# First layer's gated convolution in row form, with the token shift done by transfers inside the chip

## The reference, cut to what matters

```
h = rms_norm(x, pre_norm[i]);  proj = h @ w_in[i]
x_in, gate_b, gate_c = split(proj[:, :4608], 3)      # 1536 channels each
u    = gate_c * x_in
conv[s, c] = sum over k = 0..2 of u[s - 2 + k, c] * w[c, k]    # u of tokens before 0 is 0
tok_out = gate_b * conv
cross_out = cross-attention of the tokens into mem (512 channels)
branch = concat(tok_out, cross_out) * silu(gate)
x = x + rms_norm(branch @ w_out[i], post_norm[i])
```

## Time and profile before

| what | value |
|---|---|
| median of three executions | 956.55 us |
| profiled execution | 955.9 us, span 954.1 us |
| TensorE busy | 943.2 us (99%) |
| VectorE busy | 630.6 us (66%) |
| ScalarE busy | 474.9 us (50%) |
| DMA queue of SyncE | 59.8% of 16 engines' span |
| chain that ended last | TensorE 98% of the span |
| mixer's matmuls | from 110 to 376 us of the span |
| output projection of the first layer | from 380 to 467 us |

### The profile page before, as it was taken

How to read it: one execution, slowest core, us unless ns; L and a number is a source line. 1 busy time by engine, 2 the same in 40 slices (tenths; PEclk the granted TensorE clock), 3 DMA queues, 4 the chain that set the end, 5 groups by cost and what they waited for, 6 DMA issues and landing times.

```text
span 954.1 us, 14081 instructions
## 1 busy us (share of the span) xinstructions
PE 943.2 (99%) x5148; PEld 810.9 (85%) x5148; DVE 630.6 (66%) x868; ACT 474.9 (50%) x726; POOL 1.2 (0%) x9
## 2 busy tenths in 40 slices
PE   8999999999999999999999999999999999999996
PEld 7888888888888888888888888888888888888885
DVE  5877665666666666655595546457878778886555
ACT  6767544444444443344465355345465465464541
POOL 0000000000000000000000000000000000000000
PEclk9999999999999999999999999999999999999998
DMA  9757466666666665665576646565655755746562
GB/s 337 235 168 261 153 186 197 200 191 190 191 185 194 184 191 189 208 192 190 181 230 191 196 133 208 168 201 167 202 175 160 219 167 165 218 136 212 188 192 91
DMA packets 148778, 182.31 MB, mean 191 GB/s; under 512 B 8128, under 2 KB 116992, under 8 KB 147968
## 3 DMA queue, kind: packets, MB, share of 16 engines
q1 hardware_dynamic: 147792, 177.25, 59.8%
q10 hardware_dynamic: 944, 4.49, 1.2%
HBM read 176.48 MB, written 2.10 MB: 187 GB/s over the span
## 4 chain that ended last, share of the span: by engine, by line
PE 98%; DVE 1%; DMA 0%; ACT 0%; issue 0%; DVEq 0%; SPq 0%; ACTq 0%
PE psum L370 40%; PE psum L371 20%; PE psum L431 10%; PE psum L433 10%; PE psum L432 10%; PE psum L382 1%; PE psum L450 1%; PE psum L607 1%; PE psum L475 1%; PE psum L458 1%; PE psum L383 1%; DMA raw_ring<-in_w_kv_mem_dram 0%; PE psum L579 0%; PE psum L467 0%; PE psum L590 0%; PE psum L589 0%
## 5 line engine op out<-in xcount | busy, mean ns | idle before, releaser
L370 PE MATMUL psum<-hT_split,hi_ring 128*128 128x512 f32 x1600 | 559.3, 395 | 0.0
L923 DVE TENSOR_TENSOR lo_ring<-raw_ring,hi_ring 128x1024 fp32r<-128x1024 f32 x318 | 384.9, 1223 | 247.0 <-ACT hi_ring L656 245.5
L656 ACT ACTIVATE hi_ring<-raw_ring 128x1024 fp32r<-128x1024 f32 x318 | 335.3, 1062 | 392.8 <-PE psum L371 257.4
L371 PE MATMUL psum<-hT_split,lo_ring 128*128 128x256 f32 x1600 | 444.2, 278 | 0.0
L370 PEld LDWEIGHTS psum<-hT_split,hi_ring 128*128 128x128 f32 x1600 | 300.0, 188 | 70.5 <-issue 2.0
L371 PEld LDWEIGHTS psum<-hT_split,lo_ring 128*128 128x128 f32 x1600 | 300.7, 188 | 0.1
L431 PE MATMUL psum<-hi_ring,branchT_split 128*128 128x512 f32 x256 | 99.9, 390 | 0.0
L433 PE MATMUL psum<-hi_ring,branchT_split 128*128 128x512 f32 x256 | 99.6, 389 | 0.0
L432 PE MATMUL psum<-lo_ring,branchT_split 128*128 128x512 f32 x256 | 99.6, 389 | 0.0
L433 PEld LDWEIGHTS psum<-hi_ring,branchT_split 128*128 128x128 f32 x256 | 48.0, 188 | 10.0
L431 PEld LDWEIGHTS psum<-hi_ring,branchT_split 128*128 128x128 f32 x256 | 48.1, 188 | 10.0
(11 more groups left out here) (185 smaller groups left out, 675.7 us busy)
## 6 DMA issues: line engine op xcount, KB each, us to landing
raw_ring<-in_w_in_dram SPq DMA_DIRECT2D x224, 512.0 KB, 4.5
raw_ring<-in_w_out_dram SPq DMA_DIRECT2D x64, 512.0 KB, 4.8
raw_ring<-in_w_kv_mem_dram SPq DMA_DIRECT2D x30, 512.0 KB, 4.8
layer_area<-layer_area SPq DMA_DIRECT2D x48, 64.0 KB, 3.2
stage_area<-in_mem_dram SPq DMA_DIRECT2D x8, 256.0 KB, 6.1
x_residual<-in_x_dram SPq DMA_DIRECT2D x2, 1024.0 KB, 8.4
x_residual<-in_x_dram ACTq DMA_DIRECT2D x1, 2048.0 KB, 9.9
layer_area<-in_post_norm_dram ACTq DMA_DIRECT2D x2, 1024.0 KB, 5.9
```

What stands on the lines that cost most here:

```text
L370: mm(o, hi[:, k, P * c:P * (c + 1)], X[:, kt, :], start=kt == 0, stop=False)
L371: last = mm(o[:, SEQ:], lo[:, k, P * c:P * (c + 1)], X[:, kt, 0:SEQ], start=False, stop=kt == KT - 1)
L656: run(whi[:, slot, :], raw[:, slot, :], ACT.Copy).then_inc(hi_ready, 1)
L923: V_.tensor_tensor(wlo[:, slot, :], raw[:, slot, :], whi[:, slot, :].bitcast(f32), SUB)\
```

## The change

The mixer's 24 column groups become 12 row groups of 512 columns (three passes, `MIXES`, of x, gate c, gate b, gate). The matmul count of a unit falls from 16 to 12 and the number of units stays 96. The tokens are now on partitions, so a shift by one or two tokens is a shift by one or two partitions. SyncE does it by four transfers in SBUF for each pass (`shift_tokens`): u0 to u1 one partition down and u0 to u2 two down, and the last one or two rows of the first token tile to the top of the second. They are issued after gate b's eight loads, once u0 exists. The taps now vary along the free axis: ScalarE's queue loads them to all partitions (`load_taps`, three loads of 768 KB, into `xres`). VectorE multiplies by them (`conv_before`, `conv_now`, `conv_sum`). The finished rows are turned by 8 transposes a pass (`branch_turn`) ahead of unit 3 of the next group; ScalarE copies the high part (`branch_high`) and VectorE makes the low part (`branch_low`). `cross_values(0)` moves into the first new group. The reload of `xres` moves behind the mixer, next to `gpost`. OUT0 takes its k-tiles in another order, with the last pass's channels at units 6 and 7.

```diff
-OUT_ORDER = [0, 2, 4, 6, 8, 12, 14, 10]
+OUT0_ORDER = [0, 2, 4, 6, 12, 14, 8, 10]
+MIXES = TOK_WIDTH // ACOLS
+MIX_COLS = (0, 2 * TOK_WIDTH, TOK_WIDTH, QM_COL + CROSS_WIDTH)
...
+    tap_slots = [xres_flat[:, 1536 * i:1536 * (i + 1)] for i in range(2)]
+    u0, u1, u2, b_rows = (rows(S[:, 1024 * i:1024 * (i + 1)]) for i in range(4))
... SyncE
-        with sp.Fori(0, PAIRS) as j:
-            for g, col in enumerate((0, 2 * TOK_WIDTH, TOK_WIDTH, GATE_COL)):
-                column_group(j * (4 * B_UNITS) + (U_MIX + B_UNITS * g), w_in[0], j * BCOLS + col)
+        def shift_tokens(j):
+            sp.wait_ge(bank_free, G_MIX + 4 * j + 2)
+            for by, to in ((1, u1), (2, u2)):
+                sp.dma_start(to[by:P, :, :], u0[0:P - by, :, :]).then_inc(u_shifted, 16)
+                sp.dma_start(to[0:by, 1, :], u0[P - by:P, 0, :]).then_inc(u_shifted, 16)
+        for j in range(MIXES):
+            for g, col in enumerate(MIX_COLS):
+                row_group(U_MIX + A_UNITS * (4 * j + g), w_in[0], ACOLS * j + col, in_order)
+                if g == 2:
+                    shift_tokens(j)
... TensorE
+        def branch_turn(j):
+            pe.wait_ge(b_ready, j + 1)
+            pe.wait_ge(branch_ready, j + 1)
+            for c in range(4):
+                for t in range(TT):
+                    last = nc.tensor.transpose(ps[:, 4 + c // 2, 256 * (c % 2) + P * t:256 * (c % 2) + P * (t + 1)],
+                                               b_rows[:, t, P * c:P * (c + 1)], ident)
+            last.then_inc(b_turned, 1)
+        for j in range(MIXES):
             for g in range(4):
-                column_group(j * 4 + (G_MIX + g), j * (4 * B_UNITS) + (U_MIX + B_UNITS * g),
-                             (G_MIX + g) % 2, XA)
-        pe.wait_ge(bank_free, G_VM0 + 1)
-        cross_values(0)
+                G = G_MIX + 4 * j + g
+                at = {} if g else {3: lambda: branch_turn(j - 1)} if j else {4: first_cross_values}
+                row_group(G, U_MIX + A_UNITS * (4 * j + g), G % 2, XA, in_order, at=at)
...
-                      before=branch_wait({0: PAIRS - 1, 5: PAIRS + 1}))
+                      before=branch_wait({0: MIXES, 6: MIXES + 1}),
+                      at={3: lambda: branch_turn(MIXES - 1)} if g == 0 else {})
... ScalarE
-        act.dma_start(xres, x_in[0].rearrange("(t p) d -> p t d", p=P)).then_inc(x_again, 16)
+        for j in range(2):
+            load_taps(j)
+        def branch_high(j):
+            act.wait_ge(b_turned, j + 1)
+            run(XC[:, 4 * j:4 * j + 4, 0:SEQ], ps[:, 4:6, :].rearrange("p b (h t) -> p (b h) t", h=2), ACT.Copy)\
+                .then_inc(b_hi, 1)
+                if g == 0:
+                    row_group(G, u, G % 2, x_rows, at={4: lambda: branch_high(j - 1)} if j else {})
...
+        act.wait_ge(bank_free, G_OUT0)
+        act.dma_start(xres, x_in[0].rearrange("(t p) d -> p t d", p=P)).then_inc(x_again, 16)
         act.dma_start(gpost, post_norm[0:1, :].partition_broadcast(P)[:, 0, :]).then_inc(gpost_loaded, 16)
... VectorE
+        def branch_low(j):
+            dve.wait_ge(b_hi, j + 1)
+            V_.tensor_tensor(XC[:, 4 * j:4 * j + 4, SEQ:], cross_o, XC[:, 4 * j:4 * j + 4, 0:SEQ].bitcast(f32), SUB)\
+              .then_inc(branch_ready, 1)
+        def conv_before(j):
+            dve.wait_ge(taps_loaded[j], 16)
+            dve.wait_ge(u_shifted, 64 * (j + 1))
+            st.need()
+            st.did(V_.tensor_tensor(u1, u1, tap(j, 1), MULT))
+            st.did(V_.tensor_tensor(u2, u2, tap(j, 0), MULT))
+        def conv_now(j):
+            st.did(V_.tensor_tensor(u0, u0, tap(j, 2), MULT))
+            st.need()
+            st.did(V_.tensor_tensor(u1, u1, u2, ADD))
+        def conv_sum():
+            st.need()
+            st.did(V_.tensor_tensor(u0, u0, u1, ADD))
+        for j in range(MIXES):
+            G, u = G_MIX + 4 * j, U_MIX + 4 * A_UNITS * j
+            row_group(u, at={5: lambda: branch_low(j - 1)} if j else {6: first_cross_branch})
+            row_group(u + A_UNITS)
+            dve.wait_ge(unit_done, u + 2 * A_UNITS)
+            dve.wait_ge(bank_free, G + 1)
+            V_.tensor_tensor(u0, banks((G + 1) % 2), x_rows, MULT).then_inc(bank_free, 1)
+            row_group(u + 2 * A_UNITS, at={4: lambda: conv_before(j), 5: lambda: conv_now(j), 6: conv_sum})
+            dve.wait_ge(unit_done, u + 3 * A_UNITS)
+            st.need()
+            V_.tensor_tensor(u0, banks(G % 2), u0, MULT).then_inc(bank_free, 1)
+            row_group(u + 3 * A_UNITS)
+            dve.wait_ge(unit_done, u + 4 * A_UNITS)
+            if j:
+                dve.wait_ge(b_turned, j)
+            dve.wait_ge(tanh_done, 3 + j)
+            V_.scalar_tensor_tensor(b_rows, tanh_rows, 1.0, banks((G + 3) % 2), ADD, MULT).then_inc(bank_free, 1)
+            dve.wait_ge(bank_free, G + 4)
+            V_.scalar_tensor_tensor(b_rows, b_rows, 0.5, u0, MULT, MULT).then_inc(b_ready, 1)
...
+            out_group(g, U_OUT0 + A_UNITS * g, (G_OUT0 + g) % 2,
+                      at={5: lambda: branch_low(MIXES - 1)} if g == 0 else {})
```

More of the change, by code:

```diff
@@ L45 @@
 G_MIX, U_MIX = 7, 32
[L46 to L53, removed]
+G_OUT0, U_OUT0 = 19, 128
+G_KM1, U_KM1 = 23, 160
+G_VM1, U_VM1 = 25, 168
+G_QM1, U_QM1 = 26, 176
+G_V, U_V = 28, 184
+G_PAIR, U_PAIR = 31, 208
+G_XG1, U_XG1 = 49, 280
+G_OUT1, U_OUT1 = 51, 288
 UNITS = U_OUT1 + 4 * A_UNITS
@@ L144, in build, with rows @@
     val0 = area[:, 512:1024].rearrange("p (c t) -> p c t", c=2)
-    conv = area[:, 1024:1536].rearrange("p (c t) -> p c t", c=2)
-    upad = area[:, 1536:2052].rearrange("p (c t) -> p c t", c=2)
+    def rows(a):
+        return a.rearrange("p (t c) -> p t c", t=TT)
+    xres_flat = xres.rearrange("p t d -> p (t d)")
+    tap_slots = [xres_flat[:, 1536 * i:1536 * (i + 1)] for i in range(2)]
+    x_rows, tanh_rows = rows(xres_flat[:, 3072:4096]), rows(area[:, 0:1024])
+    u0, u1, u2, b_rows = (rows(S[:, 1024 * i:1024 * (i + 1)]) for i in range(4))
     xg_flat = xgate.rearrange("p h t -> p (h t)")
@@ L209, in build @@
     tanh_done, branch_ready = sem("tanh_done"), sem("branch_ready")
+    u_shifted, taps_loaded = sem("u_shifted"), [sem(f"conv_taps_loaded{j}") for j in range(MIXES)]
+    b_ready, b_turned, b_hi = sem("branch_rows_ready"), sem("branch_rows_turned"), sem("branch_hi")
     rope_done, s_done, max_ready, exp_done = sem("rope_done"), sem("score_done"), sem("max_ready"), sem("exp_done")
@@ L626, in _ @@
                      at={2: lambda: diff_turn(PAIRS - 1), 3: lambda: diff_values(PAIRS - 1)})
-        done0 = PAIRS + 1
+        done0 = MIXES + 1
         for g in range(4):
@@ L830, in _, with last_taps @@
         cross_take(0)
-        with act.Fori(0, PAIRS) as j:
-            for g in range(4):
[L833 to L836, removed]
+        def branch_high(j):
+            act.wait_ge(b_turned, j + 1)
+            run(XC[:, 4 * j:4 * j + 4, 0:SEQ], ps[:, 4:6, :].rearrange("p b (h t) -> p (b h) t", h=2), ACT.Copy)\
+                .then_inc(b_hi, 1)
+        def last_taps():
+            act.wait_ge(bank_free, G_MIX + 3)
+            load_taps(2)
+        for j in range(MIXES):
+            for g in range(4):
+                G, u = G_MIX + 4 * j + g, U_MIX + A_UNITS * (4 * j + g)
+                if g == 0:
+                    row_group(G, u, G % 2, x_rows, at={4: lambda: branch_high(j - 1)} if j else {})
+                else:
+                    ahead(u, A_UNITS, {2: last_taps} if (j, g) == (1, 1) else {})
+                if g == 3:
+                    act.wait_ge(unit_done, u + A_UNITS)
+                    act.wait_ge(bank_free, G)
+                    run(tanh_rows, banks(G % 2), ACT.Tanh, scale=0.5).then_inc(tanh_done, 1)
+        act.wait_ge(bank_free, G_OUT0)
+        act.dma_start(xres, x_in[0].rearrange("(t p) d -> p t d", p=P)).then_inc(x_again, 16)
         act.dma_start(gpost, post_norm[0:1, :].partition_broadcast(P)[:, 0, :]).then_inc(gpost_loaded, 16)
         for g in range(4):
-            out_group(g, U_OUT0 + A_UNITS * g, (G_OUT0 + g) % 2)
+            out_group(g, U_OUT0 + A_UNITS * g, (G_OUT0 + g) % 2,
+                      at={4: lambda: branch_high(MIXES - 1)} if g == 0 else {})
         column_group(G_KM1, U_KM1, G_KM1 % 2)
@@ L1134, in _ @@
         op(silu_twice(2, xin, val0, xgate[:, 2:4, :]))
[L1137 to L1147, removed]
-            st.need()
[L1149 to L1161, removed]
-            st.need()
-            st.did(V_.scalar_tensor_tensor(val0, val0, 0.5, conv, MULT, MULT))
-            split_branch(st, val0, bass.ds(j * 2, 2))
-            assert st.n == MIX_STEPS, st.n
@@ L1166, in _, with first_cross_branch @@
[L1166 to L1172, removed]
+        cross_o = ps[:, 4:6, :].rearrange("p b (h t) -> p (b h) t", h=2)
+        def first_cross_branch():
+            dve.wait_ge(xo_done, 1)
+            op(V_.scalar_tensor_tensor(xg_flat, ps[:, 4:6, :].rearrange("p b c -> p (b c)"), 0.5, xg_flat, MULT, MULT))
```

(3 more changed lines are left out.)

43 lines of the change are left out of this document (24 added, 19 removed).

## The result

The changed kernel took 1008.23 us (median of 6), the kernel before 956.71 us beside it: ratio 1.0538, 95% interval 1.052 to 1.0555. The forecast was 992 us, range 970 to 1012. The direction and the mechanism held; the loss is 51.5 us where some 35 were forecast. The profiled execution took 1007.24 us with a span of 1005.4 us.

A forecast was written before the change was run, and what follows sets the result against it. TensorE, busy 99% of the span, bounds the kernel. 954.1 - 5.1 (matmuls) + 2.6 (transposes) + 36.6 (shift) + 1.1 (OUT0) = 989.3 us of span, corrected to 992 us; range 970 to 1012.

The forecast's parts named there:

- matmuls of the mixer: Mixer: 1152 matmuls of 512 columns at 0.2267 us, 261.2 us instead of 266.3, a gain of 5.1 us.
- a block of 8 transposes: Turn of the branch in each pass: 0.87 us of delay to the matmuls, three times, plus 2.6 us.
- landing of the shift after gate c: Each pass: 127 partitions on one engine land at 26.9 us, the second large transfer at 28.3 us.
- low part behind it: VectorE, each pass: after two multiplications (30.8), the low part of the gate group's unit 0 is ready at 32.0 us.
- TensorE's wait in a pass, start to start less a step: Between gate b's end at 21.8 us and the low part at 32.0 us, TensorE waits 10.2 us.
- lost to the clock in a pass: After the wait TensorE's first 4 us or so run at half speed: 2.0 us lost, bounds 1.0 and 3.5.
- OUT0, unit 6: TensorE asks for the last branch's low part at 17.2 us, ready at 18.3: plus 1.1 us, bounds 1.1 and 5.
- the sum: Whole kernel: 954.1 - 5.1 + 2.6 + 36.6 + 1.1 = 989.3 us of span, forecast time 992 us.
- The choice between sixteen engines and one: Shift transfers: sixteen engines would land by 9.5 us, free; one engine takes 19.9 us for 520 KB, taken with chance 0.82.
- the ring: Four-unit ring of weights in the mixer: low part comes 2.58 us later, needed 8.2 us later, so slack 5.6 us.
- The first rival: All sixteen engines carry the shift, hiding it: 955 us, up to 960 with late loads in OUT0; chance 0.13.
- The rival of half the rate: Shift on one engine at 13 GB/s: landing 20 us later, a pass costs 32 us, about 1052 us; chance 0.05.

The follow-up runs named there:

- the last two experiments: Changed kernel with the shift cut to 112 and 15 (14) partitions and OUT0's last branch one step earlier: 953.35 us; on top, residual reload one group later: 953.07 us.
- the landing in 4.8 us: Changed kernel with the whole uncut shift (127, 1, 126 and 2 partitions) issued on GpSimd's queue instead of SyncE's: 959.78 us.
- the step in size: Changed kernel with the 127-partition transfer carrying only the first token tile, 254 KB in place of 508: 974.25 us.
- the split one: Changed kernel with each large shift transfer cut into 112 partitions and the other 15 or 14: 959.25 us, ratio 1.0022.
- the idle transfer: Changed kernel with the shift cut at 112 partitions, plus an unawaited 127-partition transfer per pass on ScalarE's queue: 987.38 us; on SyncE's queue: 1013.09 us.

## Why the prediction was right, and where it was short

| step | forecast | measured |
|---|---|---|
| matmuls of the mixer | 0.2267 us a step, -5.1 us | 0.2267 us a step away from the waits |
| a block of 8 transposes | 0.87 us | 0.88 us |
| landing of the shift after gate c | 28.3 us | 31.6 us |
| low part behind it | 32.0 us | 35.7 us |
| TensorE's wait in a pass, start to start less a step | 10.2 us | 14.1, 13.8, 14.6 us |
| lost to the clock in a pass | 2.0 us | 2.1, 1.5, 2.3 us |
| OUT0, unit 6 | 1.1 us | 4.1 us and 1.7 of clock |

**Transposes.** Timeline of TensorE at the first turn of the branch: 226.32 - 225.21 - 0.23 = 0.88 us, where the line drawn through blocks of 16 and 4 gave 0.87.

```profile
225.21 1.04 PE L560 MATMUL psum<-ident,stage_area 128*128 128x128 f32 x8
226.00 0.47 PE L448 MATMUL psum<-hi_ring,hT_split 128*128 128x512 f32 x1
226.32 0.39 PE L449 MATMUL psum<-lo_ring,hT_split 128*128 128x512 f32 x1
```

Forecast and measurement of the whole form meet in the last two experiments: 954.1 - 5.1 + 2.6 = 951.6 us of span, measured 951.6 and 951.2. That they meet to the tenth is partly luck: TensorE's waits at the head of the span are 0.2 to 0.8 us longer there than in the kernel before, which the sum does not have.

**The choice between sixteen engines and one** was right, and the runs show it: the share of 0.06 at 27 GB/s, the packet counts, and 49 us back when the partition count allows sixteen. The Trainium skill's rule (DMA: Bandwidth & Descriptors, "Why a DMA increments its semaphore by 16 and not by 1") said it for 127; by it 126 has 14 engines and 122 two, and the traces agree with 959 and 981 us. The same section says that on trn2 some of GpSimd's direct copies are spread over all sixteen engines, 127 partitions among them, and the landing in 4.8 us agrees.

**The size of the loss** was short by 16 us, from two terms. Both came out just over the upper end of their bounds (16.1 us a pass in the mean for 10 to 16, 5.8 us in OUT0 for 1.1 to 5), so the total met the top of the 985 to 1008 that they add up to, and the last 4 us of the range were margin. In the passes 48.4 us were lost instead of 36.6. Of the 3.3 us by which the landing was late, 2.6 are the engine's rate: I took the sixteenth of a busy machine, 26.1 GB/s, and the step in size measured 23.1, so 22.5 us instead of 19.9. The other 0.7 us aren't assigned; SyncE's stand of 8.5 us in an issue delays the second transfer's issue and may be part of it. The tap multiplications took 1.52 to 1.57 us instead of 1.22: from the start of the first to the low part behind the second (188.81 to 191.72) it was 2.9 us instead of the 2.5 in the sum, 0.4 us more on the path. What sets them apart from the operations of 1.22 us is the operand at a stride of three elements, which I had taken as free; no run varied the stride. The clock loss was sized well, from the beginning of the span.

In OUT0 the step was right, and the value that I took stood at the wrong end of its bounds: 5.8 us were lost, 4.1 of wait and 1.7 of clock, instead of 1.1. Timeline of ScalarE there: the last high branch, then unit 8's high part, 3.76 us late.

```profile
438.15 1.01 ACT L872 ACTIVATE branchT_split<-psum 128x1024 fp32r<-128x1024 f32 x1
442.93 2.08 ACT L688 ACTIVATE hi_ring<-raw_ring 128x1024 fp32r<-128x1024 f32 x2 [3.76 <-DMA raw_ring<-in_w_out_dram]
```

In the kernel before, beside the same reload, a unit had been late by 3.84 us, and I argued it away. It was harmless there because the ring has 5.6 us of slack (in the experiment with the branch one step earlier a unit 4.94 us late cost TensorE nothing either); here the branch's low part was queued behind it with hardly any. And behind this wait of 4 us TensorE came back at the lower clock: nine steps from 446.43 to 450.18 took 3.75 us instead of 2.04.

**The first rival** (sixteen engines) priced its case at 955, up to 960 with late loads in OUT0: that kernel is the split one, 959.25 us. The rival of half the rate (13 GB/s, 1052 us) is out: the engine moved 23 to 27 GB/s.

## What to carry to other kernels

Before moving data by partitions, factor the partition count of the transfer: on SyncE's queue 127 goes over one engine, 122 over two, 126 and 112 over many, for nearly the same bytes. A cut into 112 and the rest was the whole remedy here. A slow transfer can reach the path in two ways, through who waits for it and through what is queued behind it on its engine; here the late weights alone held TensorE for 15 to 16 us a pass, and no run had the other way alone. A queue of its own did not keep the other transfers clear of it. A late load is harmless only for work with the ring's slack before it; something urgent hung behind the same load in an engine's order has none.

## What the runs showed of the hardware that I had not expected

- Between 254 and 508 KB on one engine each added byte went at 23.1 GB/s, though stretches in which the engine ran alone show 25 to 27.
- SyncE stood 8.5 us in the issue of a 2 KB transfer behind the 508 KB on one engine, 4.5 us behind 254 KB. Behind 488 KB on two engines the next issues, of 20 KB and of 2 KB, took 0.75 and 0.57 us.
- Two queues on one engine did not share it evenly: the weights had about 8 of 26 GB/s beside the idle transfer.
- A VectorE multiplication of 1024 elements took 1.52 to 1.57 us with one operand read at a stride of three elements; those without took 1.22.
